# Moving the gate rows of a fused mixer kernel off TensorE: small transfers and VectorE block transposes in place of matmul transposes

## The reference

```python
h = rms_norm(x, norm_g[l])
proj = jnp.einsum('bsd,dn->bsn', h, w_in[l])
(aq, ak, av, ai, af, ao, az,
 bcq, bk, bv, bki, bwi, bz,
 cqkv, cb, ca, cz) = jnp.split(proj, split_points, axis=-1)
h_a = mlstm_chunked(..., soft_cap(ai + m_ib[l]), soft_cap(af + m_fb[l]))
...
beta = jax.nn.sigmoid(cb.astype(jnp.float32))
g = -jnp.exp(d_a_log[l]) * jax.nn.softplus(ca + d_dt_bias[l])
o_c = gated_delta_chunked(q_c, k_c, v_c, g, beta)
...
x = x + jnp.einsum('bsm,md->bsd', y, w_out[l])
```

## Time and profile before

| | us |
|---|---|
| median of three runs | 1542.01 |
| the profiled execution | 1541.06 |
| its span | 1539.3 |
| TensorE busy | 1534.7 |
| VectorE busy | 992.9 |
| ScalarE busy | 753.1 |
| GpSimd busy | 346.3 |

### The profile page before, as it was taken

How to read it: one execution, slowest core, us unless ns; L and a number is a source line. 1 busy time by engine, 2 the same in 40 slices (tenths; PEclk the granted TensorE clock), 3 DMA queues, 4 the chain that set the end, 5 groups by cost and what they waited for, 6 DMA issues and landing times.

```text
span 1539.3 us, 18850 instructions
## 1 busy us (share of the span) xinstructions
PE 1534.7 (100%) x7008; PEld 1271.8 (83%) x7008; DVE 992.9 (64%) x1534; ACT 753.1 (49%) x1006; POOL 346.3 (22%) x587
## 2 busy tenths in 40 slices
PE   9999999999999999999999999999999999999999
PEld 7888888888888888888878888888888888888887
DVE  6647555656759855576579667675556776664554
ACT  6745444587534444554554535535346444443332
POOL 6041112230230040127410354345300120200000
PEclk9999999999999999999999999999999999999999
DMA  9886778886787685558756787899875776666674
GB/s 299 253 241 193 223 210 232 211 235 195 227 242 213 196 222 157 165 186 272 241 180 188 221 247 218 224 272 251 258 248 178 250 220 192 207 199 193 196 248 155
DMA packets 202247, 336.98 MB, mean 219 GB/s; under 512 B 48306, under 2 KB 56900, under 8 KB 201900
## 3 DMA queue, kind: packets, MB, share of 16 engines
q1 hardware_dynamic: 181468, 288.20, 61.9%
q0 software_dynamic: 20640, 47.57, 11.7%
q10 hardware_dynamic: 48, 0.02, 0.0%
HBM read 312.03 MB, written 23.49 MB: 218 GB/s over the span
## 4 chain that ended last, share of the span: by engine, by line
PE 98%; DVE 1%; ACT 1%; issue 0%; DMA 0%; DVEq 0%
PE acc L1028 31%; PE acc L1031 31%; PE acc L1030 31%; PE mix L1091 1%; PE mix L1164 1%; PE mix L1153 0%; PE mix L1084 0%; PE mix L999 0%; PE acc L1232 0%; DVE w_lo L1639 0%; ACT w_hi L1302 0%; PE mix L1150 0%; PE mix L1140 0%; PE mix L1138 0%; DMA xs<-in_x_dram 0%
## 5 line engine op out<-in xcount | busy, mean ns | idle before, releaser
L1639 DVE TENSOR_TENSOR w_lo<-w_raw,w_hi 128x1024 fp32r<-128x1024 f32 (+2 forms) x535 | 645.7, 1217 | 422.5 <-ACT w_hi L1302 418.9
L1302 ACT ACTIVATE w_hi<-w_raw 128x1024 fp32r<-128x1024 f32 (+2 forms) x535 | 556.4, 1050 | 528.8 <-PE acc L1031 453.5
L1028 PE MATMUL acc<-w_hi,op_hi 128*128 128x512 f32 (+1 forms) x2036 | 800.0, 393 | 0.3 <-DVE w_lo L1639 0.3
L1031 PE MATMUL acc<-w_hi,op_lo 128*128 128x512 f32 (+1 forms) x2036 | 792.9, 389 | 0.0
L1030 PE MATMUL acc<-w_lo,op_hi 128*128 128x512 f32 (+1 forms) x2036 | 791.9, 389 | 0.0
L1031 PEld LDWEIGHTS acc<-w_hi,op_lo 128*128 128x128 f32 x2036 | 382.1, 188 | 80.3
L1028 PEld LDWEIGHTS acc<-w_hi,op_hi 128*128 128x128 f32 x2036 | 382.4, 188 | 79.8 <-issue 1.3
L1030 PEld LDWEIGHTS acc<-w_lo,op_hi 128*128 128x128 f32 x2036 | 382.4, 188 | 77.7
L772 POOL DMA_DIRECT2D conv_dram<-y x48 | 30.7, 696 | 171.5 <-ACT y L1354 170.7
L772 POOL DMA_DIRECT2D y_dram<-y x32 | 20.5, 711 | 182.0 <-DVE y L2078 115.0
L926 POOL DMA_DIRECT2D bp_dram<-b_ps x48 | 31.4, 705 | 71.1 <-ACT b_ps L1523 66.9
(11 more groups left out here) (336 smaller groups left out, 967.3 us busy)
## 6 DMA issues: line engine op xcount, KB each, us to landing
w_raw<-in_w_in_dram SPq DMA_DIRECT2D x367, 512.0 KB, 4.5
w_raw<-in_w_out_dram SPq DMA_DIRECT2D x128, 512.0 KB, 4.2
w_raw<-in_w_in_dram SPq DMA_DIRECT2D x16, 384.0 KB, 3.4
w_raw<-in_a_wuq_dram SPq DMA_DIRECT2D x12, 512.0 KB, 6.0
conv_dram<-y POOLq DMA_DIRECT2D x48, 64.0 KB, 3.8
y<-conv_dram POOLq DMA_DIRECT2D x48, 64.0 KB, 4.9
w_raw<-in_a_wuqi_dram SPq DMA_DIRECT2D x6, 512.0 KB, 4.7
bp_dram<-b_ps POOLq DMA_DIRECT2D x48, 64.0 KB, 4.0
```

Of the source, the lines that this page charges most:

```text
L1028: nc.tensor.matmul(o, hi[:, kt, tok], hv[:, i, n0:n1], start=(kt == (kts if late else blk["kts"])[0]), stop=False)
L1031: last_mm = nc.tensor.matmul(o, lo[:, kt, tok], hv[:, i, n0:n1], start=False, stop=(kt == blk["kts"][-1]))
L1302: func(split_ap(w_hi, c), w_raw[:, c % RAW_BUFS, 0:n], ACT.Copy).then_inc(hi_ready, 1)
L1639: vec.tensor_tensor(split_ap(w_lo, c), w_raw[:, c % RAW_BUFS, 0:n], split_ap(w_hi, c).bitcast(F32), ALU.subtract).then_inc(lo_ready, 1)
```

## The change

- **Columns to rows.** A new piece `gs` (gap 112, VectorE) clears a tile `gates5` and transposes the 32x32 blocks of `small` in place. SyncE then writes the blocks to DRAM with 4 transfers (`gates_keep`, right behind `weights(120)`), and reads them back as `rows` with 4 (`gates_bring`, behind `weights(122)`). `gt` is ScalarE's part alone and works from `rows`.
- **Rows to columns.** SyncE writes five rows to DRAM with 5 transfers (`rows_keep`, behind `weights(132)`), waits for all of them, and reads them back with 8 (`rows_bring`, behind `weights(133)`). `gb` waits on VectorE for these, does two block transposes and three copies into `gcol`, and goes on as before.
- **Places.** `gt`, `g1`, `g2`, `g3`, `g4`, `gb` stood in gaps 120, 122, 124, 126, 128, 130. They stand in 119, 120, 121, 122, 124, 129. `ce 0` to `ce 7` stay in 121 to 128. All that comes after (`ca 0` to `yd 13`) is two gaps earlier. `evac 7` is in gap 129 instead of 127.
- TensorE loses 17 transposes and three uses of its spare PSUM banks. Four start-up semaphores become two; their waits are the same.

```diff
-USES = {"par": 2, "gt": 2, "gb": 1, "kx": 1, "cn": 1, "cg": 2, "cm": 1, "cu": 1,
+USES = {"par": 2, "kx": 1, "cn": 1, "cg": 2, "cm": 1, "cu": 1,
...
-        woven[last[b] if b else FIRST_EVAC].append(("evac", b))
+        late = 2 if x["kind"] == "silu" and x["arg"] == W_A + W_B else 0
+        woven[last[b] + late if b else FIRST_EVAC].append(("evac", b))
...
-    g_end = weave(max(at, end("gates", 512) + 2), [(name, 0) for name in ("gt", "g1", "g2", "g3", "g4", "gb")], 2)
+    gates = end("gates", 512)
+    for name, slot in (("gs", 1), ("gt", 8), ("g1", 9), ("g2", 10), ("g3", 11), ("g4", 13), ("gb", 18)):
+        weave(gates + slot, [(name, 0)])
+    g_end = gates + 19
...
+            def gates_keep():
+
+                sp.wait_ge(g_dve, 1)
+                for i in range(4):
+                    sp.dma_start(g_dram[:, :, i, :], small[32 * i:32 * i + 32, :, 0:32]).then_inc(g_kept, 16)
+
+            def gates_bring():
+
+                sp.wait_ge(g_kept, 16 * 4)
+                for r, g in ((0, G_AI), (1, G_AF), (3, G_CB), (2, G_CA)):
+                    sp.dma_start(rows[:, r, :], g_dram[g:g + 8].rearrange("c m i t -> c (m i t)")).then_inc(g_moved, 16)
+
+            def rows_keep():
+
+                sp.wait_ge(g_rows, 2)
+                for q, r in enumerate((2, 3, 0, 4)):
+                    sp.dma_start(gr_dram[q], rows[:, r, :]).then_inc(g_kept, 16)
+                sp.dma_start(gr_dram[4][:, 0:P], rows[:, 5, 0:P]).then_inc(g_kept, 16)
+
+            def rows_bring():
+
+                sp.wait_ge(g_kept, 16 * (4 + 5))
+                for i in range(4):
+                    sp.dma_start(small[32 * i:32 * i + 32, :, 0:32],
+                                 gr_dram[0:4].rearrange("q c (m i t) -> (q c) m i t", m=M, i=4)[:, :, i, :]
+                                 ).then_inc(g_moved, 16)
+                    sp.dma_start(gates5[32 * i:32 * i + 8, :], gr_dram[4][:, 32 * i:32 * i + 32]).then_inc(g_moved, 16)
+
+            g_at = {name: c for c, slot in enumerate(woven) for name, _, _ in slot if name in ("gs", "g4")}
+            ahead = RAW_BUFS + AHEAD
+            small_moves = {g_at["gs"] + ahead + 1: gates_keep, g_at["gs"] + ahead + 3: gates_bring,
+                           g_at["g4"] + ahead + 1: rows_keep, g_at["g4"] + ahead + 2: rows_bring}
...
+            def gs(_, use):
+                wait_stored(dve, "gates", 512)
+                step(vec.memset(gates5[:], 0.0))
+                vec.transpose(small[:, :, 0:32], small[:, :, 0:32]).then_inc(g_dve, 1)
+
             def gb(_, use):
-                wait_filled(dve, use)
-                done_bank(vec.tensor_copy(gcol[:].rearrange("p a b -> p (a b)"), bank(use)[:, 0:72]), use)
-                dve.wait_ge(emptied[use % 4], use // 4 + 1)
+                dve.wait_ge(g_moved, 16 * (4 + 8))
+                step(vec.transpose(small[:, :, 0:32], small[:, :, 0:32]))
+                step(vec.transpose(gates5[:], gates5[:]))
+                vec.tensor_copy(gcol[:, 4, :], gates5[:, 0:8])
+                for i, q in ((0, 0), (5, 2)):
+                    ins = vec.tensor_copy(gcol[:, i:i + 4, :].rearrange("p (q m) c -> p q m c", m=M),
+                                          small[:, :, 8 * q:8 * q + 16].rearrange("p m (q c) -> p q m c", c=8))
+                step(ins)
                 vec.tensor_scalar(gder[:, 0:2, :], gcol[:, 0:2, :], -1.0, None, ALU.mult).then_inc(g_cols, 1)
```

More of the change, by code:

```diff
@@ L1041, in _ @@
             pe_done = [0]
[L1043 to L1060, removed]
             def kx(_, use):
@@ L1197, in par_columns @@
                 end_fill(turn(bank(use + 1)[:, 0:N_TAP], tap_in[0:N_TAP, :], N_TAP), use + 1)
-            pieces = dict(par=par_columns, gt=gt, gb=gb, kx=kx, cn=cn, cg=cg, cm=cm, cu=cu,
+            pieces = dict(par=par_columns, kx=kx, cn=cn, cg=cg, cm=cm, cu=cu,
                           cs=cs, cr=cr, co=co, bsc=bsc, bs=bs, bo=bo, ae=ae, ap=ap)
@@ L1359, in gt @@
             def gt(_, use):
-                wait_filled(act, use)
+                act.wait_ge(g_moved, 16 * 4)
                 act.wait_ge(head_ready, 1)
-                b = bank(use)
-                func(rows[:, 0, :], b[0:8, 0:SEQ], ACT.Tanh, bias=hcol[:, 4:5], scale=1 / GATE_CAP).then_inc(g_act, 1)
-                done_bank(func(rows[:, 1, :], b[0:8, SEQ:2 * SEQ], ACT.Tanh, bias=hcol[:, 5:6],
-                               scale=1 / GATE_CAP), use)
-                act.wait_ge(emptied[use % 4], use // 4 + 1)
-                func(rows[:, 1, :], rows[:, 1, :], ACT.Exp, scale=-GATE_CAP)
-                wait_filled(act, use + 1)
-                b = bank(use + 1)
-                func(rows[:, 3, :], b[0:8, 0:SEQ], ACT.Exp, scale=-1.0).then_inc(g_act, 1)
-                ins = func(rows[:, 2, :], b[0:8, SEQ:2 * SEQ], ACT.Identity, bias=hcol[:, 3:4])
-                done_bank(ins, use + 1)
-                act.wait_ge(emptied[(use + 1) % 4], (use + 1) // 4 + 1)
+                func(rows[:, 0, :], rows[:, 0, :], ACT.Tanh, bias=hcol[:, 4:5], scale=1 / GATE_CAP).then_inc(g_act, 1)
+                step(func(rows[:, 1, :], rows[:, 1, :], ACT.Tanh, bias=hcol[:, 5:6], scale=1 / GATE_CAP))
+                step(func(rows[:, 1, :], rows[:, 1, :], ACT.Exp, scale=-GATE_CAP))
+                func(rows[:, 3, :], rows[:, 3, :], ACT.Exp, scale=-1.0).then_inc(g_act, 1)
+                step(func(rows[:, 2, :], rows[:, 2, :], ACT.Identity, bias=hcol[:, 3:4]))
                 func(rows[:, 1, :], rows[:, 1, :], ACT.Ln, bias=1.0).then_inc(g_act, 1)
             def g2(_, use):
-                act.wait_ge(g_dve, 1)
+                act.wait_ge(g_dve, 2)
                 step(func(rows[:, 4, :], rows[:, 4, :], ACT.Exp, scale=-1.0))
@@ L2105, in par_columns @@
                     done_bank(vec.tensor_copy(par[:, c0:c0 + n], bank(use + i)[:, 0:n]), use + i)
-            pieces = dict(par=par_columns, evac=evac, g1=g1, g3=g3, gb=gb, kn=kn, kr=kr, kd=kd, kx=kx, cd=cd, conv=conv, vd=vd, csq=csq, ce=ce, ca=ca, cg=cg, cl=cl, ut=ut, ckt=ckt, cm=cm, cu=cu, cs=cs,
+            pieces = dict(par=par_columns, evac=evac, gs=gs, g1=g1, g3=g3, gb=gb, kn=kn, kr=kr, kd=kd, kx=kx, cd=cd, conv=conv, vd=vd, csq=csq, ce=ce, ca=ca, cg=cg, cl=cl, ut=ut, ckt=ckt, cm=cm, cu=cu, cs=cs,
                           co=co, cy=cy, bn=bn, bt=bt, bkn=bkn, bkt=bkt, bit=bit, bqn=bqn, bqt=bqt, bsc=bsc, btk=btk, bts=bts, bs=bs, bpt=bpt, bo=bo, at=at, ae=ae, ap=ap, ay=ay,
```

44 lines of the change are left out of this document (24 added, 20 removed).

## The result

| | us |
|---|---|
| kernel before, same chip, median of 6 runs | 1541.95 (1540.40 to 1542.68) |
| changed kernel, median of 6 runs | 1550.37 (1548.17 to 1552.32) |
| ratio | 1.0055, 95% interval 1.0045 to 1.0064 |
| its profiled execution, and span | 1549.25, 1547.5 |

The change costs 8.4 us by the medians and 8.2 us between the two profiled executions. The forecast was 1550.2.

What follows compares the result with a forecast made beforehand. TensorE was taken to bound the kernel, busy 1534.7 of 1539.3 us. Waits from closed-up gate pieces, net of savings (+3.9), and the rows' way back (+4.3) made +8.2 on 1542.0: 1550.2 us, range 1544.5 to 1557.

Steps and rivals of the forecast that it cites:

- The first part: `gt` to `g3` close up, so TensorE waits at chunks 124 to 126; less the transposes and wait removed, +3.9 us.
- step 1: `gt` in gap 119 ends at 346.94 and delays chunk 123's `w_hi`; the `w_lo` lead falls from 6.0 to 0.25 us.
- the 2.4 us that the change removes: TensorE's 8 transposes (0.90 us), 9 transposes (0.88) and the wait at 369.93 (0.61), all on the path.
- The second part: Rows return through DRAM at 383.2, so `gb` delays TensorE from chunk 133 on: +4.3 us.
- The last term: Behind `gb`, 0.6 us added for the small lead with which `kn` and `vd` are met.
- SyncE's late weights: SyncE's wait makes weights of chunks 134 and 135 some two gaps late; costed at nothing beside the wait for `gb`.
- the rows' way in: Transfers of `small` to `rows` before `gt`: landed by 337, needed at 343.4, so costed at nothing.
- The lead covers everything: Rival, chance 0.11: chunk 123's `w_hi` stays near 342 and the lead near 6 us, giving 1539.6 us.
- The way back is hidden: Rival, chance 0.17: small transfers land in 2.4 to 3 us each, only the first part counts, giving 1545.9 us.
- The waits make more of themselves: Rival, chance 0.17: TensorE's clock halves after its waits, the second chunk behind them slow, or transfers run long: 1553 to 1559.
- The table loads: ScalarE's four loads in the gate chain cost 1.28 us each; counting the skill's drain would add 5.5 us.

Runs made afterwards that it cites:

- Experiment 2: Kernel before, with TensorE's transposes and no transfers, but the gate pieces in the changed kernel's close order and `evac 7` two gaps later: 1548.42 us, ratio 1.0042.
- experiment 1: Changed kernel with the front pieces further apart (`gt` in gap 117, `g1` 119, `g2` and `g3` 122), transfers kept: 1545.35 us, ratio 1.0023.
- experiment 7: Changed kernel with `ce 0` ahead of `g2` in gap 121: 1547.72 us, ratio 1.0036.
- experiment 5: Changed kernel with GpSimd's four broadcasts held until SyncE's five stores of the rows have landed: 1549.68 us, ratio 1.0052.
- experiment 3: Changed kernel with `gb` two gaps later (131) and what follows as far apart as before: 1549.37 us, ratio 1.0047.
- experiment 4: Changed kernel with front pieces apart (`gt` 117, `g1` 119, `g2` and `g3` 123, `g4` 125) and `gb` in 131: 1543.03 us, ratio 1.0010.
- experiment 10: Changed kernel with only the way in by transfers, the way back by TensorE's nine transposes, gate pieces further apart: 1541.41 us, ratio 0.9996.
- experiment 6: Changed kernel with GpSimd's four broadcasts held until the rows are loaded back, not only stored: 1550.58 us, ratio 1.0052.

## Why the prediction was right

**The first part.** The steps of the close order held one by one. From the starts of the chunks:

| chunk | forecast, us lost | measured |
|---|---|---|
| 123 | 0 (lead 0.25) | 0.24 (349.93 against 349.46 + 0.23) |
| 124 | 0.6 | 0.83 (353.48 - 349.93 - 2.72) |
| 125 | 2.4 | 2.47 (358.67 - 353.48 - 2.72) |
| 126 | 3.3 | 3.24 (364.63 - 358.67 - 2.72) |
| sum | 6.3 | 6.8 |

The `w_lo` ends were forecast at 352.85, 357.97 and 363.96, and TensorE started at 353.48, 358.67 and 364.63, each 0.6 to 0.7 later. That constant shift comes from step 1: `gt` ended at 347.57 and not at 346.94. Experiment 2 shows that the order does this with no transfer at all, experiment 1 that without it 5.0 us are gone, experiment 7 that chunk 125 hangs on ScalarE's chain. Less the 2.4 us that the change removes, the changed kernel is 4.5 us behind the one before at chunk 132, where 3.9 was forecast.

**The second part.** Its sum was right (from chunk 132 to chunk 148 the changed kernel falls back by another 4.2 us; forecast 4.3) and its terms were not:

| term | forecast | measured |
|---|---|---|
| stores issued by | 369.7 | 371.31 |
| until the first load | 5 | 6.05 |
| issue of 8 loads | 3.5 | 4.5 |
| last issue to rows back | 5 | 1.1 |
| rows back at | 383.2 | 383.03 |
| lost at chunk 133 | 2.3 | 1.35 (386.62 - 364.63 - 7 x 2.72 - 1.6) |
| lost at chunk 134 | 1.4 | 1.40 (390.74 - 386.62 - 2.72) |
| lost later | 0.6 | the 1.06 us wait at 405.09 |

That 383.2 was met is luck: the landing of the loads was taken 3.9 us too long, the rest 3.7 too short. The 8 KB loads are fast when the queues are quiet (1.1 us) and took 4.7 in experiment 5, with the broadcasts among them; the forecast had put the collision on both pairs of moves, and it hits one. The last term was too small because of what VectorE has there: from 389.46 it is busy without a break until 401.5 (its timeline has the transposes of `cT`, the masks and `kn`), so the lead that `gb` cost is not made good. A wait of 1.05 to 1.10 us like it is in experiments 1 and 3 to 7 too, in each kernel whose rows come back by DRAM, and not in experiment 2. In experiment 3 `gb` itself waits for nothing; there the late weights had taken the lead.

**The total.** At chunk 148 the changed kernel is 8.7 us further back than at chunk 118 (8.9 against 0.2), and the forecast counted 8.2 up to there. From chunk 202 to the end it wins 0.7 us again, over many chunks, which no run here explains. That the two profiled executions then differ by 8.2, the very forecast, is luck by half a microsecond.

**A term at nothing: SyncE's late weights.** In the changed kernel it held. The weights of chunk 134, issued at 381.93 behind the small loads, landed at 385.66, and ScalarE, held by `gb` and `ca 0`, wanted them at 388.39. The 3.42 us that ScalarE waits at 375.65 are for weights issued ahead of the stores (experiment 4). But the reason given, 4 gaps of lead, is thin: with `gb` two gaps later the same weights cost the wait at chunk 134 (0.76 us, experiment 3), and in experiment 4 they leave TensorE without a lead at chunk 135. The term is nothing only while `gb` is later still. Another term at nothing, the rows' way in, was some 2 us too short and cost nothing with `gt` where the change has it: its rows land at 338.7 to 339.6 in experiments 1, 4 and 10, where 337 was the forecast.

**The rivals.** "The lead covers everything" fell: the lead was 0.25 us or less, and chunk 123 already starts 0.24 us late. "The way back is hidden" fell with VectorE's 5.05 us. "The waits make more of themselves" is half right: the clock does fall in the changed kernel, for about two thirds of a chunk, but not where the prediction put it: the slow chunk is 125, directly behind the first long wait, and no second chunk behind the waits was slow. And there its 1.6 us were taken out of the next wait (1.35 us where the forecast had 3.3), and the chunk started when its `w_lo` was there in either case. In experiments 2 and 7 the slow stretch came behind the last wait of the group, with none to hide in. In experiment 6 a wait of 3.25 us left the clock at full. That the changed kernel's runs spread over 4.2 us, and those of the kernel before over 2.3, may be this clock; it was only argued.

**What was won.** The transposes removed gave 1.8 us by the starts of the chunks: from chunk 119 to 121 it takes 6.79 us in experiment 2 and 5.89 in the changed kernel, and from 129 to 131 6.32 and 5.44. No run takes them off and changes nothing else, and in the times they can hardly be seen: change less experiment 2 is 1550.37 - 1548.42 = 2.0 us, where the second part (4.3) less the transposes is 2.5 by the forecast. The table loads: as 342.44 + 1.28 = 343.72 and the Activate at 343.73 show, a switch costs its load and no more, so the drain of 1.38 us that the Trainium skill gives in "ScalarE: Activation LUTs", section "What ACT_TABLE_LOAD costs", doesn't appear in this case, and the sum without it was the right one.

**Not tried:** the way back on another queue than the weights', fewer and larger loads, and the `w_hi` put ahead of ScalarE's part of `gb`. Each takes away one of the waits shown, and all of them together could bring at best the 2.4 us that the change removes.
